# New written orders, 128-row broadcasts, one-pass gates and packed 64x64 inverses in a two-block decoder

## The reference, cut to what matters

```python
# mLSTM: two gates per head, four heads
i_pre, f_pre = proj[..., 2048:2052], proj[..., 2052:2056]
log_i, log_f = i_pre + igate_b, log_sigmoid(f_pre + fgate_b)
# gated delta rule, per chunk and head (a_strict: beta k.k^T exp(decay differences), below the diagonal)
t_mat = a_strict + eye(c)
sol = triangular_solve(t_mat, rhs, lower=True, unit_diagonal=True)
# banded layer
q = rms_norm(h @ wq) ; k = rms_norm(h @ wk)   # per head of 64
p = sink_softmax(concat(s_meta, s_band))      # window of 128, 16 meta tokens for all
```

## Time and profile before

| what | value |
|---|---|
| median of three runs | 1686.4 us (1683.46 to 1686.85) |
| the profiled execution, its own time | 1684.41 us |
| its span, first to last instruction | 1682.6 us |
| mean granted TensorE clock | 0.969 of full |
| TensorE matmul busy | 1538.8 us (91%) |
| VectorE busy | 1190.9 us (71%) |
| ScalarE busy | 858.2 us (51%) |
| GpSimd busy | 364.1 us (22%) |
| DMA | 419.56 MB, mean 249 GB/s |

### The profile page before, as it was taken

How to read it: one execution, slowest core, us unless ns; L and a number is a source line. 1 busy time by engine, 2 the same in 40 slices (tenths; PEclk the granted TensorE clock), 3 DMA queues, 4 the chain that set the end, 5 groups by cost and what they waited for, 6 DMA issues and landing times.

```text
span 1682.6 us, 23795 instructions
## 1 busy us (share of the span) xinstructions
PE 1538.8 (91%) x9208; PEld 1177.4 (70%) x9208; DVE 1190.9 (71%) x2379; ACT 858.2 (51%) x1690; POOL 364.1 (22%) x319
## 2 busy tenths in 40 slices
PE   7999999789887988979787999999999999999999
PEld 6899998344243443434222588898999988699999
DVE  6797766676867778777656678857776556777764
ACT  5657752534545446454434565335554436565542
POOL 2010001355453535445433101301000110010000
PEclk9999999899999999999999999999999999799999
DMA  7333452999999999999999632123444542145544
GB/s 279 126 125 126 151 211 93 413 392 413 427 427 426 404 426 426 424 427 399 428 427 426 291 126 101 51 76 128 174 176 151 178 148 103 49 151 178 196 158 146
DMA packets 64336, 419.56 MB, mean 249 GB/s; under 512 B 8160, under 2 KB 12512, under 8 KB 16608
## 3 DMA queue, kind: packets, MB, share of 16 engines
q0 software_dynamic: 36864, 268.45, 38.3%
q1 hardware_dynamic: 27072, 148.54, 24.6%
q10 hardware_dynamic: 288, 1.05, 0.2%
HBM read 416.96 MB, written 1.05 MB: 248 GB/s over the span
## 4 chain that ended last, share of the span: by engine, by line
PE 63%; DMA 19%; DVE 12%; ACT 4%; issue 1%; POOL 1%; DVEq 0%; POOLq 0%
PE bank L428 62%; DMA uv<-in_uv,idx 18%; DVE lows L499 3%; DVE uv L1579 2%; PE bank L433 1%; ACT acts L440 1%; ACT L440 1%; POOL uv L1728 1%; ACT dg L440 1%; POOL sqT L635 0%; ACT wp L436 0%; DVE cacc L444 0%; DVE t L806 0%; DMA slabs<-in_w_in 0%; DVE cva L444 0%
## 5 line engine op out<-in xcount | busy, mean ns | idle before, releaser
L428 PE MATMUL bank<-uv,dg 128*128 128x512 f32 x1024 | 499.8, 628 | 84.5 <-ACT dg L440 84.4
L428 PEld LDWEIGHTS bank<-uv,dg 128*128 128x128 f32 x1024 | 189.1, 197 | 363.7 <-ACT dg L440 188.8
L1579 DVE CUSTOM_DVE_ANT_0 uv<-uv,htok 128x1024 f32<-128x1024 f32 x256 | 313.1, 1225 | 155.4 <-DMA uv<-in_uv,idx 152.6
L1728 POOL DMA_INDIRECT uv<-in_uv,idx x256 | 299.1, 1168 | 421.1 <-PE bank L428 322.2
L428 PE MATMUL bank<-hn,lows 128*128 128x272 f32 (+2 forms) x704 | 200.9, 285 | 0.0
L499 DVE TENSOR_TENSOR lows<-slabs,wp 128x2048 fp32r<-128x2048 f32 (+1 forms) x75 | 162.4, 2166 | 38.5 <-ACT wp L436 38.2
L440 ACT ACTIVATE acts<-acts,rcol 128x1 f32<-128x1 f32 x256 | 74.2, 290 | 198.1 <-DVE acts L1579 197.4
L436 ACT ACTIVATE wp<-slabs 128x2048 fp32r<-128x2048 f32 (+1 forms) x75 | 134.9, 1799 | 68.2 <-DMA slabs<-in_dn 33.1
L428 PE MATMUL bank<-hn,whl 128*128 128x272 f32 (+2 forms) x768 | 142.1, 286 | 0.0
L635 POOL TENSOR_TENSOR sqT<-sqT 128x272 f32<-128x272 f32 (+1 forms) x35 | 36.1, 1030 | 472.0 <-ACT sqT L440 470.2
L440 ACT ACTIVATE dg<-con,acts 128x128 f32<-128x128 f32 x256 | 102.8, 402 | 60.5 <-PE bank L428 53.3
(11 more groups left out here) (413 smaller groups left out, 2933.1 us busy)
## 6 DMA issues: line engine op xcount, KB each, us to landing
slabs<-in_up SPq DMA_DIRECT2D x44, 1024.0 KB, 4.8
slabs<-in_w_in SPq DMA_DIRECT2D x28, 1024.0 KB, 4.9
slabs<-in_dn SPq DMA_DIRECT2D x32, 704.0 KB, 4.1
slabs<-in_wkv SPq DMA_DIRECT2D x8, 1024.0 KB, 4.8
slabs<-in_w_out SPq DMA_DIRECT2D x8, 1024.0 KB, 4.8
slabs<-in_pq SPq DMA_DIRECT2D x7, 1024.0 KB, 9.4
slabs<-in_wq SPq DMA_DIRECT2D x4, 1024.0 KB, 4.8
slabs<-in_wo SPq DMA_DIRECT2D x4, 1024.0 KB, 4.8
```

What stands on the lines that cost most here:

```text
L428: ins = T.e.matmul(pr[2] if len(pr) > 2 else out, pr[0], pr[1], start=(start and k == 0), stop=(stop and k == len(pairs) - 1), skip_group_ ...
L1579: V.e.tensor_tensor_reduce(u_, u_, htok[:, n, :], 1.0, 0.0, ALU.mult, ALU.add, acts[:, n, e_:e_ + 1]).then_inc(*V.up("dot", q))
L1728: G.e.indirect_dma_start(uv[q % NU][:, :], None, d["uv"][:, :], bass.IndirectOffsetOnAxis(ap=idx[:, n, e_:e_ + 1], axis=0)).then_inc(s_uv[ ...
```

## The change

1. All three order texts are replaced. The items are the same; their places differ throughout. The stream of slabs is unchanged.
2. The gate weights are laid out as [128, 2, 8, 4] (kind, channel tile, head). `gate_pair` takes 36 columns from a flat view, so one product per channel tile gives one kind on output rows 0 to 3 and the other on rows 32 to 35. The columns between hold weights of other tiles, whose results nobody reads.
3. `rows`, `rows2`, `nrm` and `nk` have 128 partitions in place of 4. GpSimd fills with zeros those that are broadcast, once, and the broadcasts now have 128 input rows. The readers and writers of the four rows wait for the fill.
4. For the two chunks of 128 tokens the levels 0 to 5 work inside two 64x64 diagonal halves. The parts are packed in 64 columns per head: GpSimd, ScalarE and VectorE handle 128x256 in place of 128x512, and each product is 8 matmuls of 64x64 (4 heads, two halves: rows 0 to 63 to output rows 0 to 63, rows 64 to 127 to output rows 64 to 127 of the same bank). Level 6 computes the one off-diagonal 64x64 block. The chunk of 16 tokens is as before. The final product splits in two per head.
5. Waits are added: a broadcast of the decay for heads 0 and 3 waits for the root of the norm, some waits name what was implied by the order before, and the write of the third convolution tile waits for the eight scaled tiles of the final norm, whose scale shares the buffer.

The diff, cut to its core:

```diff
 MIX2_ORDER = """
-pj.w_in2.6.0 unit.0.1 dcols.0.0 pj.w_in2.6.1 unit.0.2 unit.1.0 unit.0.3 unit.1.1 unit.0.4 unit.1.2 ev.w_in2.6.0
...
+unit.1.0 pj.w_in2.6.0 dcols.0.0 unit.0.1 pj.w_in2.6.1 unit.0.2 ev.w_in2.6.0 unit.0.3 unit.1.1 unit.1.2 bd.0.0 unit.1.3
...
 MIX_ORDER = """
-mlstm.1.0 mlstm.0.0 mlstm.2.0 mlstm.0.2 mlstm.1.1 mlstm.0.3 mlstm.2.2 mlstm.2.3 mlstm.1.2 stick.4.12 mlstm.2.1
...
+mlstm.2.0 mlstm.0.0 mlstm.0.2 mlstm.0.3 mlstm.2.2 mlstm.2.3 pj.w_in.8.0 mem.0 mlstm.0.1 stick.1.11 mlstm.1.0
...
 SWA_ORDER = """
-pj.sk.0.0 pj.sk.0.1 pj.sv.0.0 kn.flush.0 kn.root.0 kn.rcp.0 pj.sv.0.1 pj.sv.0.2 sq.0.0 kn.bc.0 sq.0.3 sq.0.1 kn.scl.0
...
+pj.sk.0.0 pj.sk.0.1 pj.sv.0.0 pj.sv.0.1 kn.flush.0 kn.root.0 kn.rcp.0 pj.sv.0.2 sq.0.0 sq.0.3 sq.0.1 sq.0.2 sq.0.4
...
-            rows = sbuf(ph, "rows", [4, 8, T1])
+            rows = sbuf(ph, "rows", [P, 8, T1])
...
         def bsel(h):
-            return C("sel", h * P, h * P + P)[0:4, :]
+            return C("sel", h * P, h * P + P)
...
+        def gate_pair(g, c):
+            return g[:, :, :, :].rearrange("p a c h -> p (a c h)")[:, 4 * c:4 * c + 36]
+        def by_gate(x):
+            return x.unsqueeze(1).unsqueeze(3).to_broadcast([P, 2, 8, 4])
...
-            for half in range(2):
-                ins = mm(B[3][0:4, half * T1:half * T1 + T1], [(gates1[:, c, 4 * half:4 * half + 4], XR[:, c, :]) for c in range(NC)])
-                ins.then_inc(*T.up("gates", half))
+            mm(B[3][0:36, 0:T1], [(gate_pair(gates1, c), XR[:, c, :]) for c in range(NC)]).then_inc(*T.up("gates"))
...
+            G.e.memset(mrow, 0.0).then_inc(*G.up("mrow_zero"))
...
+        HALVES = (slice(0, 64), slice(64, P))
+        def packed(bank):
+            return bank[:, 0:256].rearrange("p (h i) -> p h i", h=4)
...
+                        mm(B[6][0:36, 16:T2], [(gate_pair(gates2f, c), XR[:, c, :]) for c in range(NC)])
+                        mm(B[6][0:36, 0:16], [(gate_pair(gates2, c), xT[:, c, 0:16]) for c in range(NC)]).then_inc(*T.up("gates2"))
...
+                else:
+                    T.wait_ge(*A.at("uroot", h // 3))
                 T.wait_ge(*V.at("decay", 2))
-                mm(B[2 + h][:, 0:T2], [(bsel(h), bd)]).then_inc(*T.up("bd", h))
+                mm(B[2 + h][:, 0:T2], [(bsel(h), rows2[:, 2, :])]).then_inc(*T.up("bd", h))
...
+            elif ci and 7 <= s < CSTEPS[ci] - 6:
+                l, k = 1 + (s - 7) // 4, (s - 7) % 4
+                if k == 0:
+                    T.wait_ge(*(A.at("X", ci) if l == 1 else V.at("XT", ci, l - 1)))
+                    T.wait_ge(*G.at("Q", ci, l))
+                    for h in range(4):
+                        for r in HALVES:
+                            ins = mm(b1[r, 64 * h:64 * h + 64], [(Q4[r, l % 2, h, 0:64], X[r, h, 0:64])])
+                    ins.then_inc(*T.up("QX", ci, l))
+                elif k == 2:
+                    T.wait_ge(*A.at("Y", ci, l))
+                    for h in range(4):
+                        for r in HALVES:
+                            ins = mm(b0[r, 64 * h:64 * h + 64], [(Y4[r, h, 0:64], XT[r, h, 0:64])])
...
+            elif ci and CSTEPS[ci] - 6 <= s < CSTEPS[ci] - 2:
+                up, lo, k = HALVES[0], HALVES[1], (s - 7) % 4
+                if k == 0:
...
+                        ins = mm(b1[lo, 64 * h:64 * h + 64], [(AT[ci][up, h, 64:P], X[up, h, 0:64])])
...
+                        ins = mm(b0[up, 64 * h:64 * h + 64], [(Y4[lo, h, 0:64], XT[lo, h, 0:64])])
...
+                elif k == 3 and ci:
+                    V.wait_ge(*T.at("XY", ci, l))
+                    V.e.tensor_tensor(X[:, :, 0:64], X[:, :, 0:64], packed(b1), ALU.subtract).then_inc(*V.up("X", ci, l))
+                    V.e.tensor_tensor(XT[:, :, 0:64], XT[:, :, 0:64], packed(b0), ALU.subtract).then_inc(*V.up("XT", ci, l))
...
+                    if ci:
+                        mm(o, [(XX[ci][0:64, 1, h, :], Vb[ci][0:64, h, :])], True, False)
+                        ins = mm(br[64:P, h * P:h * P + P], [(XX[ci][64:P, 1, h, 0:64], Vb[ci][64:P, h, :])], False, True)
...
+            G.wait_ge(*T.at("an0", "sum"))
+            G.wait_ge(*V.at("gates2_f"))
+            G.e.memset(rows2[:, :, :], 0.0).then_inc(*G.up("rows_zero"))
+            G.e.memset(nrm[:, :, :], 0.0).then_inc(*G.up("nrm_zero"))
...
+            G.e.memset(nk_[:, :], 0.0).then_inc(*G.up("nk_zero"))
```

More of the change, by code:

```diff
@@ new lines @@
+pj.w_in2.12.0 ev.w_in2.11.1 chunk.1.28 chunk.0.18 chunk.2.28 chunk.2.29 chunk.1.29 chunk.0.19 ev.w_in2.12.0 chunk.2.30
+chunk.2.31 chunk.1.30 chunk.1.31 pj.w_in2.13.0 low.14.0 xs.6.0 high.15.0 chunk.0.20 rec.0.1 chunk.1.32 chunk.2.32
+pj.w_in2.12.1 low.15.0 rec.0.2 rec.0.3 rec.1.0 qe.0.0 pj.w_in2.13.1 rec.0.4 ev.w_in2.12.1 rec.1.1 ev.w_in2.13.0
+rec.1.2 rec.1.3 part.2.0 part.0.0 pj.w_out2.0.0 xs.3.0 ev.w_in2.13.1 rec.2.0 part.1.0 part.3.0 rec.1.4 pj.w_out2.0.1
+rec.2.1 high.16.0 rec.2.2 pj.w_out2.0.2 high.17.0 ev.w_out2.0.0 low.16.0 rec.2.3 rec.2.4 pj.w_out2.0.3 out.0.0 out.0.1
@@ L1846, in build @@
         MIX2 = order_of(MIX2_ORDER)
[L1847 removed]
+        be, gg, bd, tmp2, sp_ = (rows2[0:4, i, :] for i in range(5))
+        nrm4 = nrm[0:4, :, :]
         ea4 = cols[0:4, 0, 4, 0:1]
[L1849 removed]
+        LV = C("lvl").rearrange("p (l i) -> p l i", l=6)
+        HALVES = (slice(0, 64), slice(64, P))
         CBANK = [(B[6], B[7]), (B[2], B[3]), (B[4], B[5])]
@@ L2124, in chunk_scalar @@
                 A.wait_ge(*T.at("trX", ci))
-                copyA(XX[ci][:, 0, :, :], heads(b0, ln)).then_inc(*A.up("X", ci))
+                if ci:
+                    copyA(XX[ci][:, 0, :, 0:64], packed(b0)).then_inc(*A.up("X", ci))
+                else:
+                    copyA(XX[ci][:, 0, :, :], heads(b0, ln)).then_inc(*A.up("X", ci))
             elif 7 <= s < CSTEPS[ci] - 2:
@@ L2129, in chunk_scalar @@
                     A.wait_ge(*T.at("QX", ci, l))
-                    copyA(Yb[ci][:, :, :], heads(b1, ln)).then_inc(*A.up("Y", ci, l))
+                    if ci:
+                        r = HALVES[1] if l == 6 else slice(0, P)
+                        copyA(Yb[ci][r, :, 0:64], packed(b1)[r, :, :]).then_inc(*A.up("Y", ci, l))
+                    else:
+                        copyA(Yb[ci][:, :, :], heads(b1, ln)).then_inc(*A.up("Y", ci, l))
             elif s == CSTEPS[ci] - 1:
@@ L2286, in side2_vector @@
                     V.wait_ge(*T.at("an0", "sum"))
+                    if c == 3:
+                        for q in range(NC):
+                            V.wait_ge(*V.at("nf", "n", q))
                     V.e.tensor_tensor(sqT[:, c, :], b, cva[:, k, :], ALU.mult).then_inc(*V.up("ev", "w_in2", i, j))
@@ L3154, in constants @@
     put("sel", sel.reshape(4, 512))
-    lv = [((i[None, :] // (2 * q) == i[:, None] // (2 * q)) & (i[None, :] // q % 2 == 1) & (i[:, None] // q % 2 == 0)) * 1.0
-          for q in LEVELS]
+    k, j = i[:, None] % 64, i[None, 0:64]
+    lv = [((j // (2 * q) == k // (2 * q)) & (j // q % 2 == 1) & (k // q % 2 == 0)) * 1.0 for q in LEVELS[0:6]]
     put("lvl", np.concatenate(lv, 1))
+    put("id64", (j == k) * 1.0)
     m16 = np.zeros((P, 16))
```

244 lines of the change are left out of this document (139 added, 105 removed).

## The result

The changed kernel takes 1644.2 us (median of 4 runs, 1642.4 to 1648.7) against 1684.9 us beside it: a ratio of 0.976, 95% interval 0.974 to 0.979, or 40.7 us less.

A forecast was written before the change was run, and what follows sets the result against it. TensorE was taken to bound the three edited stages. The terms summed to -26.8 us, of which 0.85 was passed on: -23 from 1684.4 us gave 1661.4, or 1663.4 from the median; forecast 1662 us, range 1650 to 1677.

The forecast's parts named there:

- What bounds the kernel: Whole kernel: in the three edited stages TensorE's time is nearly the kernel's, so each us off its queue can come off.
- 0.85 of the sum: Over all terms: share of the -26.8 us taken as passed on to the kernel's time, giving -23.
- Gates, -7.4: Gates blocks of first mixer and delta mixer: one pass halves the instructions, -3.5 and -3.9 us.
- Broadcasts, -5.9: Both mixers: 128 input rows end three half-clock stretches of 3.5, 6.8 and 3.4 us, together -5.9 us.
- Packing, -10.5: Delta mixer's inverses: overlapping 64x64 halves make a product 0.59 us; -10.5 us net, bounds -12 to +5.5.
- Links, -2.0: Delta mixer's inverses: smaller VectorE, ScalarE and GpSimd steps cut TensorE's 4.95 us idle by 2.0, bounds 0 and -5.
- fills and waits, 0: GpSimd's zero fills and the added waits: hidden beside other work, cost 0; 3.6 us if the fills' cover were gone.
- Orders, -1.0: New orders on all queues: could win TensorE's idle time and half clock or lose as much; -1.0 us, bounds -12 and +8.
- rival 4: Banded layer: loses its half clock as its order now leaves no gap; 10 us more gained, 1652 us; chance 0.10.
- Rivals 1, 2 and 3: Halves take turns, 1675 us (0.16); inverse stage not shorter, 1672 (0.12); 128 rows don't hold the clock, 1667 (0.08).
- rival 5: Delta mixer's inverses: packed work stays at half clock, +27 us, 1711; chance 0.07 together with milder losses by the orders.
- What would show it: Signs: gates blocks 3.5 and 3.9 us, products within 0.6, gain 6 to 8 before gathers, 13 to 17 in delta mixer.

## Why the forecast was wrong, step by step

In short, the work was forecast nearly right as a sum, and the clock was not. Without half clock the three stages became 22.3 us shorter, where the terms for gates, packing, links and the orders' idle time make 20.9; the clock gave them 20.4 us, where the sum had 5.9.

- **What bounds the kernel.** Right: three stages in which TensorE's time is the kernel's. What I made of it was not. Having said that each us taken from TensorE can come off the end, I passed on 0.85 of the sum. No run shows such a loss in the three stages, where 22.3 us of work came out for 20.9; without the factor the sum would have been 1657.6, still 13 above.
- **Gates, -7.4.** Near: the blocks are 3.4 and 3.7 us shorter; 5.6 alone, 5 to 8 when undone. Without half clock the first mixer got 3.5 us shorter by them alone, the delta mixer 2.5 for 3.9.
- **Broadcasts, -5.9.** The mechanism was right, the term mis-sized: 12.1 alone, 14 when undone, with 5 to 6 us of uncertainty about each. I had counted three stretches of the earlier trace rows, discounted one, and left out all others; with the broadcasts alone neither mixer has any left, and from the banded layer on the clock is 0.97 for 0.96. Few rows are not the only thing that lets the clock fall: with 128 rows and packed inverses the delta mixer has up to 13.7 us at half clock in its new order and 20.5 in its old one.
- **Packing, -10.5.** Near: 9.3 alone with its links. A product is cheaper than I said (0.47 for 0.59 us), the final product dearer (3.17 us per chunk, where +0.9 for both chunks makes 1.5); these errors cancelled. Less the half clock, packing is worth 11.8 us in the delta mixer by itself and 10 when undone. The row that I took for 8 full instructions (2.00 us for 272 columns) is of 128 input rows and 4 output rows; that the halves overlap held all the same.
- **Links, -2.0; fills and waits, 0.** VectorE's time in the mixer fell by 12 us; the 5 us idle among the inverses are gone, but with the order, not with packing alone (3.7 idle of 60 there). Fills and waits cost at most 1 us: without half clock the first mixer is 278.1 us with the broadcasts alone and 277.0 before.
- **Orders, -1.0.** The step that failed most: 13.3 alone, 10 to 12 for the banded layer's order alone when undone, 11 to 12 for the delta mixer's. In the banded layer it is all clock (27.3 us at half clock became 6.8 by the orders alone); in the delta mixer the orders alone save 5.5 us of work and idle time and lose 3.4 of it again at half clock. I had the price, 10 us, from the earlier trace rows, set it aside as rival 4 at a chance of 0.10, and took -1.0, near the middle of -12 and +8, where nothing in the rows pointed to the middle: the stretch begins behind a 1.3 us wait in a part without projections, and an order is just what can move either. The wait, in the kernel before:

```profile
1441.75 0.52 PE L428 MATMUL bank<-kT,qT 64*128 64x144 f32 x4 [1.31 <-DVE st L2812]
```

- **Rivals.** Rival 4 happened, on top of everything else. Rivals 1, 2 and 3 did not. Of rival 5 a small piece is real: packed in the old order, the mixer fell to half clock for 10 us behind the inverses, a price of 5, in both profiles with that pair.
- **What would show it.** Gates and products came as said; the gain ahead of the gathers was 9.7 for 6 to 8, in the delta mixer 18 to 22 for 13 to 17, and the next layer's long piece began at 1125.7.

Put as one sum, with the numbers of the runs alone: 12.1 + 5.6 + 9.3 + 13.3. The range was too narrow at its low end because rival 4 was priced there only in part and the factor pulled the other way. Why the clock falls at one place in one execution and not in the next, behind the same instructions and the same wait, stays open.

## What to carry to other kernels

Price every half-clock stretch of TensorE as a cost of its own, worth half its length, and ask of each edit, an order's too, whether it takes away what stands ahead of it: a wait beside instructions that fill part of the array, or a group of matmuls with few input rows. Where TensorE is busy for nearly all of a stage, pass its savings on in full, and compare stages by their length less half of their time at half clock: the delta mixer then agreed within 1.1 us over five profiles that spread over 6. And time single parts of a joint change, in more than one profile, before calling a gain joint.

## What the runs showed of the hardware that I had not expected

- Matmuls with 4 input rows, some 2 to 4 us of them, are followed by half clock at several places where the same columns over 128 rows, 124 of them zero, are not: 12 us in this kernel (7 to 17), from the broadcasts alone. In the changed kernel's first mixer 4 rows did no harm in the one profile.
- Two 64x64 halves on opposite corners of the array overlap while writing one PSUM bank when they alternate: 16 instructions in 0.63 us with the tail, 0.96 when issued in turn.
- Instructions of 64/128 and 64/64 in alternation cost three times the full ones that do the same: 3.17 us for 16 against 1.05 us for 8; grouped by shape, 2.17.
- The same program varies by 14 us between executions on one chip (1639.2 to 1653.5), and its mean granted clock goes with it (0.985 to 0.973). Behind the same instructions and the same 1.8 us wait the clock fell in one profiled execution and not in another.
